# Attention in one core's encoder layer: two heads at a time, normed probabilities, masks in the bias tables

## What is computed

```python
q_na, k_na, v_na, u_s5, q_xa, gate_logits = jnp.split(h @ w_in[l], IN_SPLITS, axis=-1)
o_na = neighbourhood_attention(q_na, k_na, v_na, na_rpb[l])      # 8 heads of 64, window 8 x 16 on an 8 x 64 grid
o_s5 = s5_bidirectional(u_s5, ...)                               # state space layer, GELU, GLU
o_xa = memory_cross_attention(q_xa, rms_norm(mem) @ w_mem_kv)    # 4 heads of 64, 256 memory tokens
merged = gates[0] * (o_na @ w_br_na) + gates[1] * (o_s5 @ w_br_s5) + gates[2] * (o_xa @ w_br_xa)
x = x + merged @ w_out
x = x + hierarchical_moe(rms_norm(x), ...)                       # 16 experts, 2 a token
```

## Time and profile before

| | us |
|---|---|
| median of 3 runs (lowest, highest) | 735.66 (733.75, 737.59) |
| the profiled execution | 734.23 |
| its span in the profile | 732.6 |
| TensorE busy | 643.4 (88%) |
| VectorE busy | 417.0 (57%) |
| ScalarE busy | 333.8 (46%) |
| POOL busy | 192.1 (26%) |
| DMA, mean | 157 GB/s |

### The profile page before, as it was taken

One profiled execution on the slowest core, in us unless ns is written; L12 is line 12 of the kernel. 1 busy time (PEld: TensorE's weight loads), 2 busy tenths in 40 slices (PEclk: granted clock), 3 DMA queues, 4 the chain that ended last, 5 costly groups with the idle time before them and its releaser, 6 DMA issues.

```text
span 732.6 us, 9196 instructions
## 1 busy us (share of the span) xinstructions
PE 643.4 (88%) x3197; PEld 510.7 (70%) x3197; DVE 417.0 (57%) x783; ACT 333.8 (46%) x565; POOL 192.1 (26%) x191
## 2 busy tenths in 40 slices
PE   2996999989999999999999997999287999999930
PEld 2785888869777766777778785788266877777720
DVE  4988112780475453433652249522866889888814
ACT  4873321221443423434322327322356888888722
POOL 3519921980000000000000000001545424566320
PEclk9999989999999999999999999999588999999975
DMA  9973203221412221111122223624699999999655
GB/s 293 191 166 102 72 30 87 67 78 38 108 58 85 58 58 59 55 33 59 57 83 62 82 89 103 253 110 167 247 349 388 313 340 376 366 357 347 175 87 229
DMA packets 88625, 114.96 MB, mean 157 GB/s; under 512 B 18278, under 2 KB 65480, under 8 KB 88584
## 3 DMA queue, kind: packets, MB, share of 16 engines
q1 hardware_dynamic: 76776, 93.13, 37.8%
q0 software_dynamic: 6848, 18.60, 10.7%
q10 hardware_dynamic: 4960, 2.70, 1.3%
HBM read 102.08 MB, written 15.80 MB: 161 GB/s over the span
## 4 chain that ended last, share of the span: by engine, by line
PE 55%; DMA 19%; DVE 14%; issue 6%; ACT 3%; POOL 2%; SPq 1%; ACTq 0%; DVEq 0%; POOLq 0%
DMA acc_scratch<-ysb,idx 15%; PE bank L1416 13%; PE bank L1418 12%; PE bank L1417 12%; PE bank L1603 3%; PE bank L1575 3%; DVE w_lo L908 2%; PE bank L1592 2%; PE bank L1537 1%; DMA xg<-h_scratch,idx 1%; PE bank L1709 1%; PE bank L1502 1%; POOL tok_scratch L2002 1%; PE bank L1579 1%; ACT w_hi L530 1%
## 5 line engine op out<-in xcount | busy, mean ns | idle before, releaser
L908 DVE TENSOR_TENSOR w_lo<-raw,w_hi 128x1024 fp32r<-128x1024 f32 x55 | 71.3, 1299 | 134.5 <-ACT w_hi L530 134.0
L1416 PE MATMUL bank<-h_hi,w_hi 128*128 128x512 f32 x320 | 133.7, 418 | 3.7 <-DVE w_lo L908 2.4
L1418 PE MATMUL bank<-h_hi,w_lo 128*128 128x512 f32 x320 | 127.3, 398 | 0.0
L1417 PE MATMUL bank<-h_lo,w_hi 128*128 128x512 f32 x320 | 127.1, 397 | 0.0
L1344 DVE TENSOR_TENSOR e_lo<-eraw,e_hi 128x2048 fp32r<-128x2048 f32 x48 | 108.8, 2288 | 18.1 <-ACT e_hi L805 18.1
L805 ACT CAST e_hi<-eraw 128x2048 fp32r<-128x2048 f32 x48 | 91.8, 1917 | 8.9 <-PE bank L1418 5.3
L1955 POOL TENSOR_TENSOR wcf<-wcf,prt 128x160 f32<-128x160 f32 x1 | 0.5, 457 | 308.9 <-DMA wcf<-in_moe_w_fine 308.9
L1416 PEld LDWEIGHTS bank<-h_hi,w_hi 128*128 128x128 f32 x320 | 61.8, 193 | 17.1 <-DVE w_lo L908 2.6
L530 ACT CAST w_hi<-raw 128x1024 fp32r<-128x1024 f32 x55 | 57.6, 1046 | 34.5 <-PE bank L1418 34.5
L1418 PEld LDWEIGHTS bank<-h_hi,w_lo 128*128 128x128 f32 x320 | 61.3, 192 | 13.9
L1417 PEld LDWEIGHTS bank<-h_lo,w_hi 128*128 128x128 f32 x320 | 61.6, 192 | 11.1
(11 more groups left out here) (377 smaller groups left out, 1312.8 us busy)
## 6 DMA issues: line engine op xcount, KB each, us to landing
raw<-in_w_in SPq DMA_DIRECT2D x40, 512.0 KB, 3.8
eraw<-in_moe_w_gate SPq DMA_DIRECT2D x32, 512.0 KB, 9.1
eraw<-in_moe_w_up SPq DMA_DIRECT2D x32, 512.0 KB, 13.3
eraw<-in_moe_w_down SPq DMA_DIRECT2D x32, 512.0 KB, 10.5
raw<-in_w_out SPq DMA_DIRECT2D x8, 512.0 KB, 3.8
x_sb<-in_x SPq DMA_DIRECT2D x4, 512.0 KB, 5.1
raw<-in_w_mem_kv SPq DMA_DIRECT2D x4, 512.0 KB, 7.5
...
```

The costliest lines, as they stand in the source:

```text
L908: dve.tensor_tensor(v(l_, o, [1, 1024]), v(raw, 1024 * (c % RAW), [1, 1024]), raw32(v(h_, o, [1, 1024])), SUB).then_inc(sem("w_lo_done"), 1)
L1416: pe.matmul(dst, w[0], x[0], start=first, stop=False)
L1417: pe.matmul(dst, w[0], x[1], start=False, stop=False)
L1418: return pe.matmul(dst, w[1], x[0], start=False, stop=last)
```

## The change

A unit becomes a pair: two neighbouring heads and one tile of queries, 8 pairs for XA and 16 for NA. Of a pair, the two heads' Q and K lie in partitions 0 to 63 and 64 to 127, and their scores go to two banks, one matmul after the other. The mask product is gone, and with it the bf16 identity; instead POOL adds the masks to the bias tables once, after the GLU: two tables for the first and the last tile of queries (ez_edge, 192 columns a head), and ez itself for the two between. The probabilities are normed before they are turned: VectorE's new `norm_p` takes the reciprocal of the sums and multiplies the probabilities in place. TensorE turns four tiles in a row. Then the values are the weights and the turned probabilities stream, so that the output comes out with head dimensions in its rows, the two heads in the two halves of one bank; VectorE copies it (`take_o`) into oxT or onT. The tiles "xat" and "nat" go; `split_hi` and `split_lo` make the two parts from oxT and onT in SBUF. The pipeline is one slot shorter at each step: slot s has scores(s), weighted(s - 2) and turn_p(s - 1). There are 26 slots in 22 chunks: one at the start of each of chunks 20 to 23, 25 to 38 and 41 to 44, and a second one in chunks 33, 36, 42 and 44, after half of the products. The last lines on ScalarE wait for the same loads under another semaphore's name.

```diff
-UNITS = XAH * NT + NAH * NT
+XA_PAIRS, PAIRS = XAH * NT // 2, (XAH + NAH) * NT // 2
...
-SLOTS = {c: 3 if n in range(4, 16) else 2 for n, c in enumerate(GATE_CHUNKS[:-4])}
-TURNS = {C_XAP - 2 + j: (j,) for j in range(2)} | {C_NAP - 4 + j: (j,) for j in range(4)}
-assert sum(SLOTS.values()) >= UNITS + 4
+SLOT_CHUNKS = [*range(C_S5G, C_GLU), *range(C_GLU + 1, C_XAP), *range(C_NAG, C_NAP - 4)]
+DOUBLE = (C_XAG + 2, C_XAG + 5, C_NAG + 1, C_NAG + 3)
+SLOTS = {c: 2 if c in DOUBLE else 1 for c in SLOT_CHUNKS}
+assert sum(SLOTS.values()) >= PAIRS + 2
+SPLITS = {C_XAP - 2 + j: ("xa", j) for j in range(2)} | {C_NAP - 4 + j: ("na", j) for j in range(4)}
...
-BY_DVE = ("gv", "s5p", "xap", "nap", "xat", "nat")
+BY_DVE = ("gv", "s5p", "xap", "nap")
...
+def pair(p):
+
+    if p < XA_PAIRS:
+        return False, p % (XAH // 2), p // (XAH // 2)
+    p -= XA_PAIRS
+    return True, p % (NAH // 2), p // (NAH // 2)
...
+    EDGE = 192
+    ez_edge = [at("ez_first", R0 + 16, NAH * EDGE), at("ez_last", R0 + 22, NAH * EDGE)]
...
-    ssb = at("ssb", R0 + 40, 3 * 256)
-    pr = at("pr", R0 + 43, 3 * 256)
+    onT = at("onT", R0 + 32, 4 * SEQ)
+    ssb = at("ssb", R0 + 40, 2 * 256)
+    pr = at("pr", R0 + 42, 4 * 256)
     pts = at("pts", R0 + 46, 2 * 256)
-    onx = at("onx", 132.5, NT * 256)
+    oxT = at("oxT", 132.5, 2 * SEQ)
...
+        def exp(p):
+
+            na, _, i = pair(p)
+            act.wait_ge(sem("smax"), p + 1)
+            if p >= 2:
+                act.wait_ge(sem("p_turned"), p - 1)
             n = window(i)[1] if na else MEM
...
+            for j in range(2):
+                so = 8 * (2 * (p % 4) + j)
+                src = v(ssb, 256 * j, [1, n]) if na else pv(2 + j, 0, [1, n])
+                ins = act.activation(v(pr, 512 * (p % 2) + 256 * j, [1, n]), src, ACT.Exp, bias=v(soft, so + 1, [1, 1]),
+                                     accum_out=v(soft, so + 2, [1, 1]))
+            ins.then_inc(sem("exp"), 1)
+
+        def take_p(p):
+
+            na, _, i = pair(p)
+            act.wait_ge(sem("p_turned"), p + 1)
+            if p >= 1:
+                act.wait_ge(sem("pv"), p)
             parts = [(n, k) for k, (_, n, _) in enumerate(key_chunks(i))] if na else [(P, 0), (P, 1)]
             if parts[0][0] == parts[1][0]:
-                ins = act.copy(v(pts, 256 * (u % 2), [1, 256]), pv(4 + u % 2, 0, [1, 256]))
+                ins = act.copy(v(pts, 0, [1, 512]), pv(4 + p % 2, 0, [1, 512]))
             else:
                 for n, k in parts:
-                    ins = act.copy(v(pts, 256 * (u % 2) + P * k, [1, P], pn=n), pv(4 + u % 2, P * k, [1, P], pn=n))
+                    ins = act.copy(v(pts, P * k, [256, 2], [1, P], pn=n), pv(4 + p % 2, P * k, [256, 2], [1, P], pn=n))
             ins.then_inc(sem("p_taken"), 1)
 
         def slot(s):
-            if s < UNITS:
+            if s < PAIRS:
                 exp(s)
-            if 0 <= s - 2 < UNITS:
-                take_p(s - 2)
+            if 0 <= s - 1 < PAIRS:
+                take_p(s - 1)
...
+        def split_hi(name, m):
+
+            act.wait_ge(sem("o_took"), XA_PAIRS if name == "xa" else PAIRS)
+            dst, src = (xa_hi, oxT) if name == "xa" else (na_hi, onT)
+            act.copy(v(dst, SEQ * m, [1, SEQ]), v(src, SEQ * m, [1, SEQ])).then_inc(sem("o_hi"), 1)
...
+            if c in SPLITS:
+                split_hi(*SPLITS[c])
...
+        def smax(p):
+
+            na, m, i = pair(p)
+            dve.wait_ge(sem("qk"), p + 1)
+            so = 16 * (p % 4)
+            if p == XA_PAIRS:
+                dve.wait_ge(sem("ez_masked"), 1)
+            if p == XA_PAIRS + NAH // 2:
+                dve.wait_ge(sem("ez_masked"), 3)
+            if p > XA_PAIRS:
+                dve.wait_ge(sem("exp"), p)
+            for j in range(2):
+                h, mx = 2 * m + j, v(soft, so + 8 * j, [1, 1])
+                if na:
+                    n = window(i)[1]
+                    bias = v(ez, 256 * h, [1, n]) if 0 < i < NT - 1 else v(ez_edge[i // (NT - 1)], EDGE * h, [1, n])
+                    ins = dve.tensor_tensor_reduce(v(ssb, 256 * j, [1, n]), pv(2 + j, 0, [1, n]),
+                                                   bias, 1.0, -3e38, ADD, ALU.max, mx)
+                else:
+                    ins = dve.tensor_reduce(mx, pv(2 + j, 0, [1, MEM]), AX.X, ALU.max)
             link(ins)
...
+            dve.tensor_scalar(v(soft, so + 1, [8, 2]), v(soft, so, [8, 2]), -1.0, None, MUL).then_inc(sem("smax"), 1)
+
+        def norm_p(p):
+
+            na, _, i = pair(p)
+            dve.wait_ge(sem("exp"), p + 1)
+            so = 16 * (p % 4)
+            n = window(i)[1] if na else MEM
+            link(dve.reciprocal(v(soft, so + 3, [8, 2]), v(soft, so + 2, [8, 2])))
+            for j in range(2):
+                x = v(pr, 512 * (p % 2) + 256 * j, [1, n])
+                ins = dve.tensor_scalar(x, x, v(soft, so + 8 * j + 3, [1, 1]), None, MUL)
+            ins.then_inc(sem("p_normed"), 1)
+
+        def take_o(p):
+            na, m, i = pair(p)
+            dve.wait_ge(sem("pv"), p + 1)
+            dve.tensor_copy(v(onT if na else oxT, SEQ * m + P * i, [1, P]), pv(6 + p % 2, 0, [1, P])).then_inc(
+                sem("o_took"), 1)
 
         def slot(s):
-            if s < UNITS:
+            if 0 <= s - 1 < PAIRS:
+                norm_p(s - 1)
+            if s < PAIRS:
                 smax(s)
-            if 0 <= s - 4 < UNITS:
-                take_o(s - 4)
+            if 0 <= s - 2 < PAIRS:
+                take_o(s - 2)
...
+        def split_lo(name, m):
+
+            dve.wait_ge(sem("o_hi"), m + 1 + (2 if name == "na" else 0))
+            h_, l_, src = (xa_hi, xa_lo, oxT) if name == "xa" else (na_hi, na_lo, onT)
+            dve.tensor_tensor(v(l_, SEQ * m, [1, SEQ]), v(src, SEQ * m, [1, SEQ]), raw32(v(h_, SEQ * m, [1, SEQ])),
+                              SUB).then_inc(sem("o_lo"), 1)
...
-                    wait_taken(pe, g_of["xat", 1])
+                    pe.wait_ge(sem("o_lo"), 2)
...
-                    wait_taken(pe, g_of["nat", 3])
+                    pe.wait_ge(sem("o_lo"), 6)
...
-                n_slots = SLOTS.get(c, 0)
-                if n_slots == 2 and k == 4 or n_slots == 3 and k in (3, 6):
+                if SLOTS.get(c, 0) == 2 and k == 4:
                     slot(s)
-                    s += 1
...
+        def scores(p):
+            na, m, i = pair(p)
+            if p:
+                pe.wait_ge(sem("smax" if p > XA_PAIRS else "exp"), p)
+            for j in range(2):
+                if na:
+                    w0, n, _ = window(i)
+                    x, y = v(qT, SEQ * m + P * i, [1, P], p0=64 * j, pn=64), v(kT, SEQ * m + w0, [1, n], p0=64 * j, pn=64)
+                else:
+                    n = MEM
+                    x, y = v(qxT, SEQ * m + P * i, [1, P], p0=64 * j, pn=64), v(kmT, MEM * m, [1, n], p0=64 * j, pn=64)
+                ins = pe.matmul(pv(2 + j, 0, [1, n]), x, y, start=True, stop=True)
+            ins.then_inc(sem("qk"), 1)
+
+        def chunks_of(p):
+            na, _, i = pair(p)
             return key_chunks(i) if na else [(0, P, 0), (1, P, P)]
 
...
+        def turn_p(p):
+            pe.wait_ge(sem("p_normed"), p + 1)
+            if p >= 2:
+                pe.wait_ge(sem("p_taken"), p - 1)
+            for j in range(2):
+                for k, (_, n, a0) in enumerate(chunks_of(p)):
+                    ins = pe.transpose(pv(4 + p % 2, 256 * j + P * k, [1, P], pn=n),
+                                       v(pr, 512 * (p % 2) + 256 * j + a0, [1, n]), v(ident, 0, [1, P]))
             ins.then_inc(sem("p_turned"), 1)
 
...
+        def weighted(p):
+            na, m, _ = pair(p)
+            pe.wait_ge(sem("p_taken"), p + 1)
+            if p >= 2:
+                pe.wait_ge(sem("o_took"), p - 1)
+            for k, (w, n, _) in enumerate(chunks_of(p)):
+                for j in range(2):
+                    h = 2 * m + j
+                    vals = v(vw, NAW * w + HD * h, [1, HD], pn=n) if na else v(vm, XAW * w + HD * h, [1, HD])
+                    ins = pe.matmul(pv(6 + p % 2, 0, [1, P], p0=64 * j, pn=64), vals,
+                                    v(pts, 256 * j + P * k, [1, P], pn=n), start=k == 0, stop=k == 1)
             ins.then_inc(sem("pv"), 1)
 
         def slot(s):
-            if s < UNITS:
+            if s < PAIRS:
                 scores(s)
...
+            if 0 <= s - 2 < PAIRS:
+                weighted(s - 2)
+            if 0 <= s - 1 < PAIRS:
+                turn_p(s - 1)
 
...
-        pool.sem_inc(sem("masks"), 1)
+
+        pool.wait_ge(sem("s5_lo"), 2)
+        for edge, kind in enumerate((0, 2)):
+            off = 64 * (1 - edge)
+            pool.tensor_tensor(v(ez_edge[edge], 0, [EDGE, NAH], [1, EDGE]), v(ez, off, [256, NAH], [1, EDGE]),
+                               v(maskb, 256 * kind + off, [0, NAH], [1, EDGE]), ADD).then_inc(sem("ez_masked"), 1)
+        pool.wait_ge(sem("ez_masked"), 2)
```

(37 more changed lines are left out.)

78 lines of the change are left out of this document (2 added, 76 removed).

## The result

The changed kernel takes **800.04 us** (median of 4 runs, 795.24 to 803.56), the kernel before on the same chip 734.70 (4 runs, 732.18 to 737.59): a ratio of 1.089, 95% interval 1.085 to 1.093. It is slower, as forecast, and within the range, but 20 us above the 780 that were named. The profiled execution took 798.70 us with a span of 797.0; before it was 734.23 and 732.6. So 64.5 us are to be explained where the sum had 46.4.

What follows compares the result with a forecast made beforehand. TensorE was taken to bound chunks 20 to 49, with new waits for norm_p: schedule 29.1 + long-wait clock 6.8 + ordinary clock 8.5 + POOL 2 = 46.4 on 734.2, named 780 us; own range 766 to 792, stated range 756 to 803.

Steps and rivals of the forecast that it cites:

- the chain: Chunk boundaries: tile take, weight cast, w_lo subtraction, then norm_p, which TensorE's transposes await; ordinary wait 2.2 us.
- T: The moment TensorE starts a chunk, at the slot that opens it; T+3.7 means 3.7 us later.
- the schedule: Chunks 20 to 49, stage by stage: 9.85 us per one-slot chunk, +29.1 us together before clock and POOL terms.
- long waits: Chunks 22, 23, 39 and 49: waits of 6.9, 5.4, 3.6 and 3.6 us, each charged 1.7 of clock, 6.8 together.
- second slots: Chunks 33, 36, 42, 44: mid-chunk slots paying only TensorE's work, taken as 2.05 us, else 2.6 without overlap.
- the clock in ordinary waits: 18 one-slot boundaries with 2.2 us waits: clock falls in a quarter to a third of them, 8.5 us.
- Rival 2: The clock falls in every ordinary wait, so 8.5 becomes 31 us: 803 us, chance 0.12.
- POOL: Chunks 25 and 26: three mask additions slow two VectorE operations by 1.0 each, +2 us, between 0 and 4.
- rival 4: A pair's heads do not run side by side, 4 x 0.55 us more: 782 us; 0.73 shared with forecast and 770 case.
- Rival 1: At T+1.5 norm_p is done before TensorE reaches the transposes, and the kernel gets faster: 704 us, chance 0.06.
- Rival 3: Clock never falls in ordinary waits and POOL disturbs nothing: 770 us; 0.73 shared with forecast and 782 case.
- Rival 5: The chain has unseen slack, half the ordinary wait goes and no clock is lost there: 752 us, chance 0.06.

Runs made afterwards that it cites:

- Experiment 4: Changed kernel with 6 unread 128x384 products filling part of TensorE's wait ahead of the transposes in slots that open a chunk (from chunk 22): 781.08 us.
- experiments 3: Changed kernel with 13 unread products of 384 columns filling TensorE's wait ahead of the transposes in slots that open a chunk: 778.69 us, ratio 1.062.
- experiment 8: Kernel before the change with one part alone, the masks added to the bias tables by POOL: 735.38 us, ratio 1.000.
- experiment 7: Changed kernel with norm_p in the same slot ahead of the next w_lo, POOL additions in 24 short ones, and splits moved earlier: 701.90 us, ratio 0.956.
- experiment 1: Changed kernel with VectorE's norm_p(s) at the end of slot s, ahead of the next w_lo: 717.93 us, ratio 0.977.

## Why the prediction was right and where it was wrong

**Right: what bounds, and the chain.** The direction rested on the order and on rows 3 and 4: norm_p ends at T+3.7, TensorE is at its door at T+1.5. The trace has T+3.72 (344.64 + 0.62) and T+1.29 (345.31 - 2.48), the wait 2.48 where 2.2 was said, 21 waits where 21 were said. Their sum is 65.7 us, above the 50 to 60 that were named; 5.7 of it are chunk 25's. Where the clock stays at 1.00, the schedule holds to two hundredths: 9.83 in chunk 28, 9.84 and 9.85 in chunk 35 of experiments 4 and 3. Chunks 39 and 49 wait for xa_lo and na_lo as named, 3.66 each.

**Right: the whole schedule.** Experiment 4 has the schedule with two clock falls in ordinary chunks. Its stretch takes 285.3 us (180.92 to 466.2). The forecast's is 246.2 + 25.5 = 271.7 without the wait of chunk 49. The 13.6 between them are chunk 25 (17.9 instead of 10.5, 7.4), the chunks with long waits, 22 with 23 and 39 (2.8 and 1.8), two ordinary falls, with chunk 20 in chunk 21, which was not filled, and in 38 (1.4 and 1.6), and shorter second slots and a shorter end of the stretch (-1.4): 13.6.

**Failed: the clock in ordinary waits, "between never and always (0 and 31) I take a quarter to a third, 8.5".** The price of one fall was right in the mean: 1.7 us was forecast. The share was not. Of the 18 ordinary waits, 13 lost clock in the profiled execution and 5 did not (chunks 21, 28, 30, 36, 42). Taken chunk by chunk against the schedule, for instance 11.41 and 11.12 against 9.85 in chunks 34 and 35 and 11.27 against 9.6 in chunk 41, they lost 22.5 us, 1.73 each in the mean; single chunks lost from about 1 to 2.8 (chunk 26). That is 14 above the term. Experiments 3 and 4 measure the same sum directly: 21 and 19 us come back when the standstill is filled or halved. The reason given for the small share, that 2.2 us "is a little shorter than the one of the two that cost", was no reason: the wait came out at 2.48, between the two. Rival 2 was nearer to the truth, with 13 of 18 instead of all.

**Failed: POOL, "Two VectorE operations in the chain at 1.0 each: +2, between 0 and 4".** Chunk 25 took 17.92 us instead of 10.5. Of the 7.4, 5.7 are the longer wait (8.59 instead of 2.9), the rest the clock behind it. The step that failed was to read row 11, where w_lo took 2.22 beside an addition, as a price of 1.0 for any VectorE operation. In rows 10 the addition runs from 136.09 to 138.49 and w_lo began at 137.35: it stood for the 1.14 us that were left and then took 1.08. What an operation loses is the rest of the POOL instruction that it meets. The first multiply of norm_p met one with 2.84 us left (236.45 to 239.29); the second, begun at 239.36, met the next and took 3.17, to 242.53, just behind that one's end (242.38). (The 2.91 in rows 10, named as an addition's, is a product's.) It is not a matter of norm_p's kind of operation: w_lo lost 2.28 in experiment 8, where more was left. The Trainium skill (SBUF — State Buffer, Who interferes with whom) says so: the shared port pair is held for a whole instruction, the other engine "fully blocks"; tensor_scalar can contend, an instruction with two inputs in SBUF does, tensor_reduce on trn2 does not. Rows agree, 6.08, 3.33 and 3.36 against 0.74. The prediction had this rule at "up to 7" and dismissed it, because the 2.22 "agrees only with a part of an instruction"; it was the part that was left.

**Small terms.** The pair runs side by side in full: scores of both heads in 0.63, values of both in 0.59 (341.54 to 342.17 in the timeline above; 371.80 to 372.39), a second slot 1.8 (11.66 less 9.85) where 2.05 was taken, so chunks 36 and 42 come out at 11.66 and 11.64 instead of 11.9 and rival 4 falls. The long waits lost about the clock that was charged: chunks 22 to 24 took 36.8 us where it was 37.05 with it, 39 and 40 took 17.1 where it was 17.0. Behind chunk 49 the rest is 3.5 us longer, where nothing was forecast beyond the clock's 1.7.

**The account.** Forecast 46.4; ordinary clock +14.0; chunk 25 +5.4; start and end of the stretch +1.1; what is left is -2.5, mostly the 1.7 of chunk 49's clock, which lies in the end already, and the second slots: 64.4 of 64.5.

**What was luck.** The 800 us lie outside of the forecast's own range (766 to 792). They lie within the stated one only because that was drawn out to rival 2's 803. That rival comes within 3 us of the measurement, but not by its mechanism alone: its 31 us of clock were 22.5, and POOL's 5.4 above the term fill most of the gap.

**Rivals.** Rival 1 was wrong for this kernel and right for its neighbour: with norm_p in time it gave 216 us for the stretch and 704 in all; experiment 7 has 213.7 and 701.9. What it named as the point of decision, norm_p done in time, is what experiment 1 brings about. Rival 3 (770) took the chain without ordinary clock loss and POOL's hold at nothing; experiments 3 and 4, with that hold still in, are at 779 and 781. Rival 5 finds nothing for it: the ordinary waits came out longer than forecast, not half as long.
